# Second block's MLPs fed by the stream times the norm's weight, with the sum of squares and the root taken later and the squared root applied to the down projection

## The reference, cut to what matters

```python
def rms_norm_2(x, g):
    xf = x.astype(jnp.float32)
    xf = xf * lax.rsqrt(jnp.mean(xf * xf, axis=-1, keepdims=True) + EPS)
    return (xf * g.astype(jnp.float32)).astype(x.dtype)

h = h + merged @ w_o[l]
hn = rms_norm_2(h, norm2_g[l])
h = h + jnp.square(jax.nn.relu(hn @ w_mlp_up[l])) @ w_mlp_down[l]
```

## Time and profile before

| what | value |
|---|---|
| time, median of 3 runs | 3077.1 us (3072.35 to 3080.65) |
| span of the profiled execution | 3078.2 us |
| PE busy | 3009.2 us, 98% of the span |
| PE weight loads busy | 2627.8 us, 85% |
| DVE, ACT, POOL busy | 60%, 48%, 36% |
| mean granted clock of TensorE | 0.990 |

### The profile page before, as it was taken

The page is one execution under the profiler, slowest core; times in us unless marked ns, Lnnn a source line. Parts: engine busy times, 40 slices in busy tenths (PEclk is TensorE's granted clock), DMA queues, the critical chain, the costliest instruction groups (busy, mean ns, idle before and its releaser), DMA issues.

```text
span 3078.2 us, 49499 instructions
## 1 busy us (share of the span) xinstructions
PE 3009.2 (98%) x20284; PEld 2627.8 (85%) x20284; DVE 1838.9 (60%) x3263; ACT 1474.6 (48%) x2497; POOL 1102.2 (36%) x428
## 2 busy tenths in 40 slices
PE   7999999999999999999999999999999999999999
PEld 5888887877788886799999877888999978879999
DVE  2777775566675546576465465664465366654654
ACT  3453333454533325565465446654365356654553
POOL 0422222000322231255455423444545423435554
PEclk9999999999999999999999999999999999999999
DMA  7545652211456732278355433334555533335554
GB/s 250 200 153 194 202 191 91 74 56 42 137 202 241 253 115 65 60 258 270 122 165 181 149 110 87 113 104 137 178 161 169 156 98 110 105 115 165 165 191 137
DMA packets 404560, 459.90 MB, mean 149 GB/s; under 512 B 8688, under 2 KB 381424, under 8 KB 404336
## 3 DMA queue, kind: packets, MB, share of 16 engines
q1 hardware_dynamic: 401248, 453.32, 45.7%
q10 hardware_dynamic: 3088, 3.42, 0.3%
HBM read 455.66 MB, written 1.05 MB: 148 GB/s over the span
## 4 chain that ended last, share of the span: by engine, by line
PE 91%; DVE 5%; ACT 2%; issue 1%; DMA 1%; ACTq 0%; POOL 0%; DVEq 0%
PE bank L445 25%; PE bank L447 24%; PE bank L446 24%; PE banks L445 1%; PE banks L447 1%; PE banks L446 1%; PE banks L2585 1%; PE bank L1456 1%; PE bank L649 1%; PE banks L1467 1%; PE banks L2598 1%; DVE wl L405 1%; DMA X<-in_ctxT 1%; PE bank L2546 1%; PE banks L1804 1%
## 5 line engine op out<-in xcount | busy, mean ns | idle before, releaser
L420 POOL TENSOR_TENSOR wl<-raw,wh 128x768 fp32r<-128x768 f32 (+3 forms) x324 | 980.2, 3026 | 1812.8 <-ACT wh L386 1812.8
L386 ACT ACTIVATE wh<-raw 128x2048 fp32r<-128x2048 f32 (+1 forms) x336 | 636.1, 1893 | 458.6 <-PE bank L447 395.9
L405 DVE TENSOR_TENSOR wl<-raw,wh 128x1280 fp32r<-128x1280 f32 (+3 forms) x332 | 495.3, 1492 | 450.1 <-ACT wh L386 449.9
L445 PE MATMUL bank<-nh,wh 128*128 128x272 f32 (+1 forms) x1712 | 506.8, 296 | 3.4 <-DVE nl L2168 2.8
L447 PE MATMUL bank<-nh,wl 128*128 128x272 f32 (+1 forms) x1712 | 494.8, 289 | 0.0
L446 PE MATMUL bank<-nl,wh 128*128 128x272 f32 (+1 forms) x1712 | 493.1, 288 | 0.0
L445 PE MATMUL bank<-xh,wh 128*128 128x512 f32 (+2 forms) x1282 | 441.0, 344 | 4.2 <-DVE xl L783 3.7
L447 PE MATMUL bank<-xh,wl 128*128 128x512 f32 (+2 forms) x1282 | 433.8, 338 | 0.0
L446 PE MATMUL bank<-xl,wh 128*128 128x512 f32 (+2 forms) x1282 | 433.6, 338 | 0.0
L445 PE MATMUL bank<-hh,wh 128*128 128x512 f32 (+1 forms) x1024 | 344.1, 336 | 0.0
L446 PE MATMUL bank<-hl,wh 128*128 128x512 f32 (+1 forms) x1024 | 344.1, 336 | 0.0
(11 more groups left out here) (470 smaller groups left out, 5614.5 us busy)
## 6 DMA issues: line engine op xcount, KB each, us to landing
raw<-in_mlp_w SPq DMA_DIRECT2D x128, 1024.0 KB, 5.6
raw<-in_w_in SPq DMA_DIRECT2D x60, 1024.0 KB, 5.2
raw<-in_mod_wT SPq DMA_DIRECT2D x48, 1024.0 KB, 5.0
extra<-in_mod_wT SPq DMA_DIRECT2D x36, 1024.0 KB, 5.4
raw<-in_w_mlp_up SPq DMA_DIRECT2D x32, 1024.0 KB, 5.4
raw<-in_w_mlp_down SPq DMA_DIRECT2D x32, 1024.0 KB, 5.1
raw<-in_w_in SPq DMA_DIRECT2D x34, 512.0 KB, 5.0
raw<-in_w_ssd_down SPq DMA_DIRECT2D x16, 1024.0 KB, 5.1
```

The costliest lines, as they stand in the source:

```text
L386: nc.scalar.activation(self.wtile(self.wh, c1), self.rawtile(c1), AF.Copy).then_inc(*up("act_wh", ("wh", c1)))
L405: nc.vector.tensor_tensor(l, r, h.bitcast(F32), ALU.subtract).then_inc(*up("dve_wl", ("wl_dve", c1), *([("wl_pool", c1)] if n == self.P[c1 ...
L420: nc.gpsimd.tensor_tensor(l, r, h.bitcast(F32), ALU.subtract).then_inc(*up("pool_wl", ("wl_pool", c1), *([] if n else [("wl_dve", c1)])))
L445: nc.tensor.matmul(o, ah, bh, start=first, stop=False)
```

## The change

In each layer of the second block, ACT and DVE make `nh` and `nl` from `X2` times the norm's weight alone, one tile behind each `o2` result. PE goes from the last `o2` group to the first up chunk; the 12 sum matmuls stand behind the first up chunk, the four spread matmuls behind the second, and the filler of this norm is gone. DVE takes the root ahead of its work for the second up chunk. ACT squares the spread root into `rv`. Each of the 32 down groups is multiplied by `rv` into a temporary and then added to `X2`. The two norms of type `n1` and all of the first block stay.

```diff
@@ pe_total is cut in two
+        self.pe_sums(name, b, T)
+        self.pe_root(name, T)
+
+    def pe_sums(self, name, b, T):
...
-        self.pe_root(name, T)
@@ pe_mlp(self, st, X, T, late=None), up chunks
+                if i == 0 and late:
+                    self.pe_sums(late, self.pe_bank((7,), "tot", late), T)
+                if i == 2 and late:
+                    self.pe_spread(late, T, (7,))
@@ act_mlp(..., late=None)
             self.act_split(c)
+            if late and p == ("m1", st, 0, 2):
+                self.act_late(late, T)
@@ act_hidden(self, st, i, T, late=None)
         if i >= 4:
             ACT.wait_ge(*at("L", st, i - 4))
+        elif late:
+            ACT.wait_ge(*at("sqadd", late, 6))
@@ dve_mlp(..., late=None)
+            if late and c == second:
+                self.dve_quarter_root(late, T)
@@ new functions
+    def act_raw2(self, name, g, l, k, T):
+        ACT.wait_ge(*at("x", name, k))
+        nc.scalar.activation(self.nh[:, k, T], self.X2[:, k, T], AF.Copy, scale=self.col(g, 8 * l + k)).then_inc(*up("act_xh", ("xh", name, k)))
+        self.act_square(name, k, self.X2[:, k, T], T)
+
+    def dve_raw2(self, name, g, l, k, T):
+        DVE.wait_ge(*at("xh", name, k))
+        nc.vector.scalar_tensor_tensor(out=self.nl[:, k, T], in0=self.X2[:, k, T], scalar=self.col(g, 8 * l + k), in1=self.nh.bitcast(F32)[:, k, T],
+                                       op0=ALU.mult, op1=ALU.subtract).then_inc(*up("dve_xl", ("xl", name, k)))
+
+    def act_late(self, name, T):
+        ACT.wait_ge(*at("rs", name))
+        nc.scalar.activation(self.rv[:, T], self.place["rsb", name][:, T], AF.Square).then_inc(*up("act_r2", ("r2", name), ("out", "rsb", name)))
+
+    def dve_resid_late(self, key, k, late, nxt, T):
+        t = self.u[4 + k % 2][:, T]
+        DVE.wait_ge(*at("acc", *key))
+        DVE.wait_ge(*at("r2", late))
+        nc.vector.tensor_tensor(t, self.place[key][:, T], self.rv[:, T], ALU.mult).then_inc(*up("dve_late", ("out", *key)))
+        DVE.wait_ge(*at("out", *key))
+        nc.vector.tensor_tensor(self.X2[:, k, T], self.X2[:, k, T], t, ALU.add).then_inc(*up("dve_x", ("added", *key), *([("x", nxt, k)] if nxt else [])))
@@ pe_merge
-        self.pe_total(f"n2{l}", T)
-        self.pe_mlp(f"up{l}", self.nparts(f"n2{l}"), T)
+        self.pe_mlp(f"up{l}", self.nparts(f"n2{l}"), T, f"n2{l}")
@@ act_merge
-                    self.act_square(f"n2{l}", square, self.X2[:, square, T], T)
+                    self.act_raw2(f"n2{l}", "norm2_g", l, square, T)
...
-        self.act_square(f"n2{l}", 7, self.X2[:, 7, T], T)
-        self.act_norm2(f"n2{l}", T)
-        self.act_mlp(f"up{l}", T, self.X2, "n11" if l == 0 else None)
+        self.act_raw2(f"n2{l}", "norm2_g", l, 7, T)
+        self.act_mlp(f"up{l}", T, self.X2, "n11" if l == 0 else None, f"n2{l}")
@@ dve_merge
-                self.dve_resid2(("o2", l, 2 * j + m), 2 * j + m, f"n2{l}", T, 0.5)
-        self.dve_norm2(f"n2{l}", "norm2_g", l, T)
+                k = 2 * j + m
+                self.dve_resid2(("o2", l, k), k, f"n2{l}", T, 0.5)
+                if k:
+                    self.dve_raw2(f"n2{l}", "norm2_g", l, k - 1, T)
+        self.dve_raw2(f"n2{l}", "norm2_g", l, 7, T)
...
-        self.dve_mlp(f"up{l}", T, lambda key, k, last: self.dve_resid2(key, k, nxt if last else None, T))
+        self.dve_mlp(f"up{l}", T, lambda key, k, last: self.dve_resid_late(key, k, f"n2{l}", nxt if last else None, T), f"n2{l}")
```

More of the change, by code:

```diff
@@ L600, in pe_total @@
             self.pe_busy(2, 2)
+        self.pe_sums(name, b, T)
+        self.pe_root(name, T)
+    def pe_sums(self, name, b, T):
+        nc, at, up, PE = self.nc, self.T.at, self.T.up, self.PE
         self.pe_eps(b, T)
@@ L803, in hidden, with pe_mlp @@
         return self.hid[st]
-    def pe_mlp(self, st, X, T):
+    def pe_mlp(self, st, X, T, late=None):
         at, PE = self.T.at, self.PE
@@ L827, in pe_mlp, with act_mlp @@
             c += 1
-    def act_mlp(self, st, T, xs=None, nxt=None):
+    def act_mlp(self, st, T, xs=None, nxt=None, late=None):
         nc, at, up, ACT = self.nc, self.T.at, self.T.up, self.ACT
@@ L847, in act_mlp @@
                 if p[0] == "m1":
-                    self.act_hidden(st, 8 * p[2] + 2 * p[3] + m, T)
+                    self.act_hidden(st, 8 * p[2] + 2 * p[3] + m, T, late)
                 elif p[2] == 3 and nxt:
@@ L855, in act_mlp, with act_hidden @@
                 self.act_fourier_high(3, square, 0)
-    def act_hidden(self, st, i, T):
+    def act_hidden(self, st, i, T, late=None):
         nc, at, up, ACT = self.nc, self.T.at, self.T.up, self.ACT
@@ L871, in act_hidden, with dve_mlp @@
         nc.scalar.activation(H[i // 8 % 2][:, i % 8, T], t, AF.Copy).then_inc(*up("act_H", ("H", st, i // 8, i % 8)))
-    def dve_mlp(self, st, T, resid):
+    def dve_mlp(self, st, T, resid, late=None):
         nc, at, up, DVE = self.nc, self.T.at, self.T.up, self.DVE
@@ L879, in dve_mlp @@
         dmods = []
+        second = self.ix["m1", st, 0, 1]
         while c < len(self.P) and (self.P[c][0][1] == st or self.P[c][0][0] == "dmod"):
@@ L2175, in dve_resid2 @@
                                        ).then_inc(*up("dve_x", ("out", *key), *([("x", nxt, k)] if nxt else [])))
+    def act_raw2(self, name, g, l, k, T):
+        nc, at, up, ACT = self.nc, self.T.at, self.T.up, self.ACT
+        ACT.wait_ge(*at("x", name, k))
+        nc.scalar.activation(self.nh[:, k, T], self.X2[:, k, T], AF.Copy, scale=self.col(g, 8 * l + k)).then_inc(*up("act_xh", ("xh", name, k)))
+        self.act_square(name, k, self.X2[:, k, T], T)
+    def dve_raw2(self, name, g, l, k, T):
+        nc, at, up, DVE = self.nc, self.T.at, self.T.up, self.DVE
+        DVE.wait_ge(*at("xh", name, k))
+        nc.vector.scalar_tensor_tensor(out=self.nl[:, k, T], in0=self.X2[:, k, T], scalar=self.col(g, 8 * l + k), in1=self.nh.bitcast(F32)[:, k, T],
+                                       op0=ALU.mult, op1=ALU.subtract).then_inc(*up("dve_xl", ("xl", name, k)))
+    def act_late(self, name, T):
+        nc, at, up, ACT = self.nc, self.T.at, self.T.up, self.ACT
+        ACT.wait_ge(*at("rs", name))
+        nc.scalar.activation(self.rv[:, T], self.place["rsb", name][:, T], AF.Square).then_inc(*up("act_r2", ("r2", name), ("out", "rsb", name)))
+    def dve_resid_late(self, key, k, late, nxt, T):
+        nc, at, up, DVE = self.nc, self.T.at, self.T.up, self.DVE
+        t = self.u[4 + k % 2][:, T]
[4 more added lines that the diff above has]
+        nc.vector.tensor_tensor(self.X2[:, k, T], self.X2[:, k, T], t, ALU.add).then_inc(*up("dve_x", ("added", *key), *([("x", nxt, k)] if nxt else [])))
     def nparts(self, name):
```

## The result

The changed kernel took 3066.18 us (median of 6 runs, 3064.49 to 3070.02) against 3077.26 us for the kernel before in the same series: ratio 0.9968, 95% interval 0.9957 to 0.9979. It is faster, by 0.32% where 0.23% had been forecast. "Faster by over 0.3%" had been given 0.31 and "within 0.3%" 0.62; the point estimate fell on the other side of that line, and the interval (0.21% to 0.43%) covers both.

What follows compares the result with a forecast made beforehand. PE bounds the kernel (91% of the last chain), standing still 12.83 us before the MLPs. Layer 0 6.43 - 2.04 - 1.1 = 3.29, layer 1 6.40 - 2.04 - 0.46 = 3.90, together 7.2: 3069.9 us, range 3063 to 3076.5.

Steps and rivals of the forecast that it cites:

- The stand-still: Between last o2 product and first up matmul, 6.43 us in layer 0 and 6.40 in layer 1: all 12.83 removed.
- The parts are in time: First up chunk, layer 1: low part of k = 7 follows at 2.3 us, 2.7 us ahead of the need at 5.0.
- The root is in time: Before the spread, behind the second up chunk: root ready at 9.9 us, PE arrives at 12.2, cover 2.3 us.
- Sums and spread: Small matmuls moved into the up stream: 0.84 us for sums and 1.20 for spread, 2.04 a layer.
- the change of kind costs the other 0.28: Fp32 matmuls between fp32r groups: 0.28 us beyond own steps, read from one 272-column matmul, taken as 0.30 per insertion.
- Rival A: More is won: change of kind hides behind the stream, sums cost 0.24; gain 9.6 us, 3067.5 us, chance 0.20.
- The tail of layer 0: End of layer 0: second DVE operations meet POOL's work, so the sums of n11 start 0.46 to 1.4 later; 1.1 taken.
- The tail of layer 1: End of the program: the last addition becomes two dependent DVE operations with POOL idle, costing 0.46 us.
- Rival B: Seam at o2's end: low parts wait for POOL splits, root late too; 2 us a layer, 3073.9 us, chance 0.14.
- Rivals C and D: C: DVE-POOL turns in down groups, 3094 us, chance 0.06; D: another wait holds first up matmul, 3077 us, 0.03.
- The forecast's own rule: About 0.3%, 9.2 us, is what measurement can tell from no change; the forecast gain of 7.2 falls short.
- own range: Whole-kernel time 3067.5 to 3071.5 us, said to follow from gains of 5.9 to 9.0.

Runs made afterwards that it cites:

- The run with the order undone: Changed kernel with sums, root, spread and fillers again ahead of the first up chunk, high and low parts still made early; one run of 3076.3 us.
- the run with the delay: Changed kernel with unused DVE multiplications ahead of tile 7's low part, 5 in layer 0, 12 in layer 1; first-up-chunk stretch grew 0.59 and 7.12 us.
- the second: Same changed kernel timed again against the kernel before: 3068.38 us against 3076.07, ratio 0.9975.

## Why the prediction was right, and where not

- **The stand-still goes, all of it: right.** 12.83 us forecast, 6.42 + 6.41 measured. The run with the order undone gives all of it back. It doesn't make the early parts worthless: they are what lets PE start, and by the estimate given there up to 1.4 us of the 6.4 would be theirs alone.
- **The parts are in time: right.** The last low part ended 2.0 us behind the first up matmul (2.3 forecast, wanted at 5.0). The steps were a little different: the low part of k = 5 delayed nothing, so the addition ended at 0.6 and not 1.3, while the low part of k = 6 took 1.03 us beside POOL's square. Timeline of DVE, layer 1:

```profile
2877.03 0.42 DVE L2189 SCALAR_TENSOR_TENSOR X<-bank,X 128x256 f32<-128x256 f32 x1 [1.32 <-PE bank L447]
2877.37 1.43 DVE L2203 SCALAR_TENSOR_TENSOR nl<-X,cols,nh 128x256 fp32r<-128x256 f32 x2
```

- **The root is in time: right.** It was ready 9.2 us behind the first up matmul (2885.98), 9.9 forecast; PE came for it at 11.9.
- **Sums and spread: mis-sized.** 2.04 a layer forecast; the two traces give 1.44 and 1.27, the run without them 1.58 and 1.49. The difference between the two readings is the first up chunk of the kernel before, which was slower by 0.14 and 0.23 us. The failed step is "the change of kind costs the other 0.28": it was drawn from one matmul with 20 stationary columns. Over both layers 1.4 us of the 1.8 by which the forecast was short. Rival A named this as a saving, with a wrong share for the sums: its 9.6 us is nearer to the 9.0 than the forecast's 7.2. The spread's own 0.90, which the forecast kept against a lower price, is right: 0.88 measured.
- **The tail of layer 0: mis-sized.** 1.1 forecast, 0.65 measured, the other 0.4 us. The forecast let POOL's split of 2424.64 go ahead of DVE's second operation of tile 6. Timeline of DVE after, and of POOL, at the place of the earlier trace rows:

```profile
2412.52 0.43 DVE L2218 TENSOR_TENSOR u<-bank,rv 128x272 f32<-128x272 f32 x1
2412.99 0.55 DVE L2220 TENSOR_TENSOR X<-X,u 128x272 f32<-128x272 f32 x1
2415.12 0.44 DVE L2218 TENSOR_TENSOR u<-bank,rv 128x272 f32<-128x272 f32 x1 [1.58 <-PE bank L447]
2415.59 0.66 DVE L2220 TENSOR_TENSOR X<-X,u 128x272 f32<-128x272 f32 x1
```
```profile
2411.48 1.76 POOL L594 TENSOR_TENSOR sq<-sq,u 128x272 f32<-128x272 f32 x1 [1.52 <-ACT u L585]
2413.20 2.03 POOL L420 TENSOR_TENSOR wl<-raw,wh 128x768 fp32r<-128x768 f32 x1
2415.20 0.76 POOL L594 TENSOR_TENSOR sq<-sq,u 128x272 f32<-128x272 f32 x1
```

  DVE asked at 2412.99 while POOL's square ran; it came next and finished at 2413.54, and POOL's split, in the queue behind the square, took 2.03 in place of 1.83. Whoever waits gets its turn between two operations of the other: in layer 1 of the changed kernel POOL's split, begun at 2886.63 behind DVE's 1.49 us split, came next in the same way, and DVE's next low part took 2.05 us.
- **The tail of layer 1: right.** 0.46 forecast, 0.49 measured.
- **Rival B** didn't come to pass, but its mechanism is there: the new low part does wait for POOL (0.64 to 1.03 us in the changed kernel, 1.98 in the run with the delay), though it is no tensor x tensor operation. By the Trainium skill ("SBUF — State Buffer", SBUF: two separate sides) an operation of DVE with two SBUF inputs and a GpSimd operation that reads SBUF exclude each other for the whole instruction; the traces agree for both kinds of operation: scalar x tensor with tensor took 1.98 us beside POOL's split and 0.5 alone, tensor x tensor 2.06 and 0.43. What kept the price at zero is that hand-overs alternate and the margin was 3 us.
- **Rivals C and D** are excluded by the stretch of layer 1's down part, 136.60 us before and after, and by the first up matmul at 0.12 us.

The terms as measured: 6.42 - 1.44 - 0.65 + 6.41 - 1.27 - 0.49 = 9.0 us, 0.29%. The forecast's own rule put "faster by over 0.3%" below one half because the sum was short of 9.2 us; with the right terms it would have been about even. That the first series shows 0.32% and the second 0.25% is scatter around 0.29%, so on which side of 0.3% the result fell was luck. And the forecast's "own range" from 3067.5 doesn't follow from its bounds: a gain of 5.9 to 9.0 gives 3068.1 to 3071.2, and 3067.5 belongs to rival A. The gain of 9.0 by the stretches lies at the upper of these bounds.

## What to carry to other kernels

A per-token factor that passes through the next product needn't be ready when the product starts: begin with what is there and apply the factor at the first place where an engine with slack touches the result. Put it where the last result of a stage doesn't pass through two operations, best into an operation that has to read PSUM anyway. The price of an operation inserted into a stream is to be taken from one of the same shape, the stationary side included, and a cover has to be counted in what can step in between, not in microseconds alone.

## What the runs showed that had not been expected

- An fp32 matmul between fp32r matmuls costs its own steps (0.43 us for 256 columns, 0.23 for 64) when its stationary side is 128 columns wide, and 0.2 to 0.3 us more when it is 20 wide. The reason is open.
- When DVE waits for POOL it gets in before POOL's next queued operation (0.55 us at 2412.99, POOL's next 2.03 in place of 1.83), and the other way round (2.05 us for DVE's low part behind POOL's split), so here the two busy engines alternate rather than starve one another.
- After 4.1 us of a standing PE the granted clock was 0.50 for about 6 us, and after the 4.5 us of idling in the kernel before without filler it cost 2.4 to 2.5 us behind the stand-still in each layer, and in layer 0 some 0.8 us within it.
- Executions of the same kernel reach layer 0's `o2` anywhere between 2196.3 and 2204.7 us. Between the two traces of the changed kernel each of the steps goes with a lower granted clock in the later one (0.85 to 0.90 against 1.00), so 6.4 us of difference in span can stand where not one instruction differs.
